# Output projection of an RG-LRU block with an expert-choice mixture: a third tile begun early, weight copies put later

## The chip, the cores and the metric

The kernel runs on one core of one Trainium2 chip. The time is that of the device, in microseconds (us), of the whole program from start to end. The engines are TensorE (PE: matmuls; PEld is its weight load), VectorE (DVE), ScalarE (ACT), GpSimd (POOL) and SyncE (SP), which here issues most of the DMA transfers. Each engine works off its own list of instructions in order, and waits on semaphores (counters) where it needs the work of another.

## What is computed

One layer: a bidirectional Griffin RG-LRU block on 1024 latent and 256 context tokens of width 1024, then an expert-choice mixture of 16 experts, then a norm. The part that matters here, cut from the reference:

```python
# rglru_mixer: g_lat, u_lat from h @ w_in; two directions of a gated linear recurrence
y_lat = 0.0
for d, reverse in enumerate(DIRECTIONS):
    ...
    y_lat = y_lat + diag_scan(jnp.exp(la_l), b_l, h_end, reverse)
out_lat = (jax.nn.gelu(g_lat) * y_lat).astype(h_lat.dtype) @ w_out      # (1024 x 1280) @ (1280 x 1024)
...
x = x + mod[:, 2] * y_lat                                               # gated residual
h = modulate(rms_norm(x, norm_ffn_g[l]), mod[:, 3], mod[:, 4])
x = x + mod[:, 5] * expert_choice_ffn(h, router_w[l], ...)              # router: softmax(h @ w_router), top 128 tokens of each expert
```

## The kernel before

Every fp32 product is made of three fp32r matmuls: high part by high part, low by high, high by low. "High" is the value rounded to fp32r (`copy` on ScalarE or a copy on GpSimd), "low" is what remains (a subtraction, mostly on VectorE).

**The mixer.** `mixer_block(n)` does channels 128n to 128n+127 (NB = 10 blocks) of all 1280 tokens: TensorE makes the input products and the gates, ScalarE the sigmoids, exp, tanh, square and square root, VectorE the convolution, the products and the scans. The result y of a block is split by `high_y` (ScalarE) and `low_y` (VectorE), and GpSimd's queue stores both to `y_scr` in HBM (`store_y`). For a block, VectorE's steps are: `i_d` times `u` for both directions (semaphore `v_done`), the w product for each direction (L960, `w_done`), `scan_input` for each (L987, `b_done`), `scans` (L994 to L1007: four scans, a sum, the product with the gelu).

**The output weight.** `a_w_out` comes as five pieces `wo_raw`, each for two blocks of channels. The high copies lie in `act_h` (four made by GpSimd, L496, `wo_h_ready`, the last by ScalarE), the low copies in `act_l`: `wo_low(i)` on VectorE (L970, semaphore `wo_l_ready`). In the list of VectorE `wo_low(0)` stands ahead of the w products of the last block, 1 and 2 behind each of them, 3 behind the scans, 4 behind the low part of the last y.

**The output projection** makes 8 tiles of 128 tokens (called tile 0 to tile 7), each in two halves of 512 columns in a PSUM bank each. `project_first` begins tiles 0 and 1, when y of eight blocks is stored: their y comes back from `y_scr` into `yt_first_h/l`. First the high products of both tiles (32 matmuls each: high y and low y by the high weight, L1392 and L1394), then the low products (high y by the low weight, 32 in all for both, L1399), then all three products of the ninth block (12 matmuls) and of the tenth (12), which takes y straight from `y_h` and `y_l`. Two `spread` matmuls put the gate row of the mixture (`gate5`) into banks 3 and 6. Tiles 2 to 7 follow in a loop, each 2 x 30 matmuls (`project_half`, L1376 to L1378), with y loaded by SP into `yt_h/l` (two slots) and x into `xt`. Between the halves of a tile stands the turning (8 transposes, L1424, `turn_tile`) of an earlier tile's normed rows, behind it the router product (16 matmuls, L1432, `route`).

For each tile VectorE gates and adds (L1030, L1032; `x2_ready`), ScalarE sums the squares and takes the root, VectorE scales (`scale_rows`, L1041, `xn2_ready`). SP's list holds per tile, in this order: store of the sum (`x_scr`), then, when the rows are scaled, store of the normed rows (`n_scr`), then the loads of the tile after the next. The loads of tile 3 stand behind the two stores of tile 0.

**The experts** stream 384 weight pieces of 1 MB, each split on ScalarE and VectorE and used by 12 matmuls.

Of the kernel before, what the change touches and what calls it, by code (L numbers as in the profile page):

```python
# [23 lines left out]
F32 = mybir.dt.float32  # L24
# [4 lines left out]
ALU = mybir.AluOpType  # L29
# [5 lines left out]
def program(nc, stack, x, c, ctx, c_ctx, ada_w, ada_b, norm_mix_g, norm_ffn_g, final_g, a_w_in, a_conv_w,  # L35
# [28 lines left out]
    def place(name, shape, dtype, kb):  # L64
# [154 lines left out]
        yt_first_loaded yt_second_loaded yt_ninth_loaded yt_loaded_a yt_loaded_b xt_loaded_a xt_loaded_b proj_done gated_done x2_ready sq2_done  # L219
        rms2_done rstd2_ready xn2_ready xn_turned h2T_ready h2T_second logits_done  # L220
# [62 lines left out]
    def wait_past(eng, signal, value):  # L283

        if not (isinstance(value, int) and value <= 0):
            eng.wait_ge(signal, value)

    with nc.Block() as block:
# [3 lines left out]
        def _(sp):  # L292
# [79 lines left out]
            def tile_loads(t, slot, early=False):  # L372
                if not early:
                    sp.wait_ge(sem["proj_done"], (t - 1) * 2)
                    sp.wait_ge(sem["x2_ready"], t - 1)
                cols = bass.ds(t * P, P)
# [4 lines left out]
                if early:  # L381
                    sp.wait_ge(sem["x2_ready"], t - 1)
                sp.dma_start(xt[slot][:], x[0, cols, :]).then_inc([sem["xt_loaded_a"], sem["xt_loaded_b"]][slot], 16)
# [14 lines left out]
            first_load(1, 1, 0, NB - 2, sem["yt_second_loaded"])  # L398
            sp.wait_ge(sem["y_stored"], 32 * (NB - 1))
# [8 lines left out]
            tile_loads(2, 0, early=True)  # L408
            tile_stores(0, 0)
            sp.wait_ge(sem["proj_done"], 4)  # L410
            tile_loads(3, 1, early=True)
# [165 lines left out]
        def _(act):  # L577
# [112 lines left out]
            def norm2(t, slot, j):  # L690
                act.wait_ge(sem["x2_ready"], t + 1)

                if j is not None:
                    act.wait_ge(n_stored[slot], j * 16)
                    act.wait_ge(sem["xn_turned"], t - 1)
                nc.scalar.activation(xn[slot][:], x2[slot][:], ACT.Square, accum_out=stat[:, 0, slot:slot + 1]).then_inc(sem["sq2_done"], 1)
                act.wait_ge(sem["sq2_done"], t + 1)
                nc.scalar.activation(stat[:, 1, slot:slot + 1], stat[:, 0, slot:slot + 1], ACT.Sqrt, scale=1.0 / D,
                                     bias=eps[:]).then_inc(sem["rms2_done"], 1)

            def modulate2(t):
                act.wait_ge(sem["xn_turned"], t + 1)
                wait_past(act, sem["logits_done"], t)
                for k in range(KD // 2):
                    last = nc.scalar.activation(h2T[:, k, :], bank(4 + k // 4)[:, (k % 4) * P:(k % 4 + 1) * P], ACT.Identity,
                                                scale=scale2[:, k:k + 1], bias=shift2[:, k:k + 1])
# [6 lines left out]
            act.wait_ge(sem["row_spread"], 4)  # L713
            for j in range(2):
                copy(gate5_row[:, j * HALF:(j + 1) * HALF], bank((3, 6)[j])).then_inc(sem["gate5_ready"], 1)
            modulate2(0)
            with act.Fori(1, NT // 2) as j:
                for slot in range(2):
                    t = j * 2 + slot
                    modulate2(t - 1)  # L720
                    norm2(t, slot, j)
# [79 lines left out]
            def squares(part):  # L801
                lo, hi = groups_fin[part]
                for t in range(lo, hi):
                    act.wait_ge(x_loaded[t], 32)
                    if t >= 2:
                        act.wait_ge(sem["squares_done"], NT + NCT + t - 1)
                    nc.scalar.activation(junk_fin[t % 2], fin[t][:], ACT.Square, accum_out=stat[:, 0, t:t + 1]).then_inc(sem["squares_done"], 1)
                act.wait_ge(sem["squares_done"], NT + NCT + hi)
# [14 lines left out]
            act.wait_ge(sem["squares_done"], NT + NCT + NT + 1)  # L823
# [5 lines left out]
        def _(dve):  # L829
# [84 lines left out]
            def mixer_block(n):  # L914
# [40 lines left out]
                if n == NB - 1:  # L955
                    wo_low(0)
                for d in range(2):
# [3 lines left out]
                    if n == NB - 1:  # L961
                        wo_low(1 + d)
# [56 lines left out]
            wo_low(3)  # L1019
            low_y(NB - 1)  # L1020
            wo_low(4)


            def residual(t, slot, j, turned=None):
                for half in range(2):
# [4 lines left out]
                    v.tensor_tensor(x2[slot][:, cols], bank(((0, 1), (2, 7))[slot][half]), gate2_row[:, cols], ALU.mult).then_inc(sem["gated_done"], 1)  # L1030
# [6 lines left out]
            def scale_rows(t, slot):  # L1037
                dve.wait_ge(sem["rms2_done"], t + 1)
                v.reciprocal(stat[:, 0, slot:slot + 1], stat[:, 1, slot:slot + 1]).then_inc(sem["rstd2_ready"], 1)
                dve.wait_ge(sem["rstd2_ready"], t + 1)  # L1040
# [598 lines left out]
```

## Time and profile before

| | us |
|---|---|
| median of 3 runs | 1716.64 (1716.53 to 1716.76) |
| profiled execution, its own time | 1717.74 |
| its span | 1716.0 |
| TensorE busy in the span | 1615.6 (94%) |
| VectorE busy | 1391.7 (81%) |
| ScalarE busy | 1212.4 (71%) |
| GpSimd busy | 223.1 (13%) |
| granted TensorE clock, mean | 0.97 |

All times below are from the span's start. The page of the profile gives totals by engine and by group of instructions; the timeline lists one engine's instructions with the idle time ahead of each and the instruction that ended it; the windows give busy time, granted clock and DMA share in a stretch. The granted clock is 1.00 at 2.4 GHz and 0.50 at 1.2 GHz.

### The profile page before, as it was taken

To read this page: it belongs to the slowest core of one execution; us is meant where nothing else is said; L and a number is where in the kernel's file an instruction comes from. 1 tells how busy PE (TensorE), PEld (TensorE's weight loads), DVE (VectorE), ACT (ScalarE), POOL (GpSimd) and SP (SyncE) were. 2 spreads that over 40 slices of the span, in tenths; PEclk is the share of its full clock that TensorE was granted. 3 is DMA by queue.
4 is the path that set the end of the run, shared out by engine and by line. 5 is a ranking of instruction groups with operands and counts; after the bars stand their busy time and mean duration, and the time that the engine had idled before them with its cause. 6 is when DMAs were issued, how large, how long until landed. Compare 5 with 4: busy or idle time off the path is not lost.

```text
span 1716.0 us, 21522 instructions
## 1 busy us (share of the span) xinstructions
PE 1615.6 (94%) x7661; PEld 1326.7 (77%) x7661; DVE 1391.7 (81%) x1115; ACT 1212.4 (71%) x1112; POOL 223.1 (13%) x154
## 2 busy tenths in 40 slices
PE   4999999997997389999999999999999999999995
PEld 1788888785886368888888888888888888888884
DVE  2777888789424879888898898988888989888896
ACT  3688888885213258778877777787777777877774
POOL 0400000003001300211202102102022021020010
PEclk9999999998998589999999999999999999999998
DMA  9323533434659169999999999999999999999995
GB/s 348 96 86 124 166 123 117 137 122 133 224 182 364 56 247 381 371 392 390 370 405 382 361 410 374 378 404 364 399 386 363 407 381 371 401 375 401 373 361 212
DMA packets 107654, 512.05 MB, mean 298 GB/s; under 512 B 11434, under 2 KB 37704, under 8 KB 56400
## 3 DMA queue, kind: packets, MB, share of 16 engines
q1 hardware_dynamic: 99968, 483.39, 72.3%
q0 software_dynamic: 7632, 27.92, 5.8%
q8 instruction: 36, 0.59, 0.1%
q14 instruction: 18, 0.15, 0.0%
HBM read 479.76 MB, written 31.52 MB: 298 GB/s over the span
## 4 chain that ended last, share of the span: by engine, by line
PE 87%; DVE 8%; SPq 2%; ACT 2%; issue 1%; DMA 0%; POOL 0%; ACTq 0%; DVEq 0%; POOLq 0%
PE psum L1500 14%; PE psum L1508 14%; PE psum L1502 14%; PE psum L1554 6%; PE psum L1561 6%; PE psum L1556 6%; PE psum L1268 5%; PE psum L1269 5%; PE psum L1270 5%; PE psum L1541 2%; PE psum L1376 2%; PE psum L1377 2%; PE psum L1378 2%; SPq L301 1%; DVE act_l L906 1%
## 5 line engine op out<-in xcount | busy, mean ns | idle before, releaser
L1155 DVE TENSOR_TENSOR part_l<-raw,part_h 128x2048 fp32r<-128x2048 f32 x380 | 847.6, 2286 | 58.0 <-ACT part_h L579 57.1
L579 ACT ACTIVATE part_h<-raw 128x2048 fp32r<-128x2048 f32 x384 | 720.7, 1917 | 165.7 <-PE psum L1508 94.8
L1500 PE MATMUL psum<-part_h,xgT_h 128*128 128x512 f32 x1024 | 287.3, 398 | 2.4 <-DVE xgT_l L1216 2.1
L1508 PE MATMUL psum<-part_l,xgT_h 128*128 128x512 f32 x1024 | 281.6, 392 | 0.1
L1502 PE MATMUL psum<-part_h,xgT_l 128*128 128x512 f32 x1024 | 281.7, 392 | 0.0
L1502 PEld LDWEIGHTS psum<-part_h,xgT_l 128*128 128x128 f32 x1024 | 194.1, 190 | 41.3
L1508 PEld LDWEIGHTS psum<-part_l,xgT_h 128*128 128x128 f32 x1024 | 193.3, 189 | 41.7 <-DVE part_l L1155 0.8
L1500 PEld LDWEIGHTS psum<-part_h,xgT_h 128*128 128x128 f32 x1024 | 191.1, 191 | 39.9 <-DVE xgT_l L1216 2.5
L1554 PE MATMUL psum<-part_h,hidT_h 128*128 128x512 f32 x512 | 157.9, 390 | 1.4 <-DVE hidT_l L1167 1.4
L1556 PE MATMUL psum<-part_h,hidT_l 128*128 128x512 f32 x512 | 157.7, 389 | 0.0
L1561 PE MATMUL psum<-part_l,hidT_h 128*128 128x512 f32 x512 | 136.9, 389 | 0.0
L539 POOL COPY id_scatter<-tok_id 128x1 int32 (+1 forms) x15 | 31.2, 2083 | 757.1 <-DVE y_out L1176 757.1
L1554 PEld LDWEIGHTS psum<-part_h,hidT_h 128*128 128x128 f32 x512 | 96.0, 188 | 21.7 <-DVE hidT_l L1167 1.8
L1561 PEld LDWEIGHTS psum<-part_l,hidT_h 128*128 128x128 f32 x512 | 96.1, 188 | 20.0
L1556 PEld LDWEIGHTS psum<-part_h,hidT_l 128*128 128x128 f32 x512 | 96.1, 188 | 19.9
L1268 PE MATMUL psum<-act_h,wu_h 128*128 128x512 f32 (+1 forms) x224 | 78.8, 352 | 1.3 <-DVE act_l L906 1.3
L579 ACT ACTIVATE hidT_h<-psum 128x512 fp32r<-128x512 f32 x64 | 35.0, 596 | 63.3 <-PE psum L1541 63.3
L1269 PE MATMUL psum<-act_h,wu_l 128*128 128x512 f32 (+1 forms) x224 | 78.8, 352 | 0.0
L1270 PE MATMUL psum<-act_l,wu_h 128*128 128x512 f32 (+1 forms) x224 | 78.7, 351 | 0.0
L1268 PE MATMUL psum<-act_h,wg_h 128*128 128x512 f32 x160 | 63.3, 396 | 0.0
L1269 PE MATMUL psum<-act_h,wg_l 128*128 128x512 f32 x160 | 62.4, 390 | 0.0
L1270 PE MATMUL psum<-act_l,wg_h 128*128 128x512 f32 x160 | 62.3, 389 | 0.0
(254 smaller groups left out, 2210.6 us busy)
## 6 DMA issues: line engine op xcount, KB each, us to landing
raw<-in_exp_w_gate_dram SPq DMA_DIRECT2D x128, 1024.0 KB, 7.1
raw<-in_exp_w_up_dram SPq DMA_DIRECT2D x128, 1024.0 KB, 6.8
raw<-in_exp_w_down_dram SPq DMA_DIRECT2D x128, 1024.0 KB, 9.4
ada_piece<-in_ada_w_dram SPq DMA_DIRECT2D x16, 1024.0 KB, 6.3
ada_buf<-in_ada_w_dram SPq DMA_DIRECT2D x8, 1024.0 KB, 12.9
u_raw<-in_a_w_in_dram SPq DMA_DIRECT2D x10, 512.0 KB, 3.8
g_raw<-in_a_w_in_dram SPq DMA_DIRECT2D x10, 512.0 KB, 8.5
y_scr<-y_h POOLq DMA_DIRECT2D x10, 512.0 KB, 3.8
```

The lines of the kernel that those rows point to most:

```text
L579: return nc.scalar.activation(dst, src, ACT.Identity)
L1155: v.tensor_tensor(part_l[slot][:], raw[slot][:], part_h[high][:].bitcast(F32), ALU.subtract).then_inc(sem["part_l_ready"], 1)
L1268: mm(out_ap, xh, wh, start=(i == 0), stop=False)
L1269: mm(out_ap, xl, wh, start=False, stop=False)
L1270: last = mm(out_ap, xh, wl, start=False, stop=(i == len(pairs) - 1))
L1376: mm(out_ap, yh, wo_h[:, n, cols], start=(n == 0), stop=False)
L1500: mm(dst, xgT_h[slot][:, i, :], wh[:, f, :], start=(i == 0), stop=False)
L1502: mm(dst, xgT_l[slot][:, i, :], wh[:, f, :], start=False, stop=False)
L1508: last = mm(dst, xgT_h[slot][:, i, :], wl[:, f, :], start=False, stop=(i == CHUNKS - 1))
L1554: mm(bank(4 + n), hh, wh[:, k, cols], start=(i == 0 and k == 0), stop=False)
L1556: mm(bank(4 + n), hl, wh[:, k, cols], start=False, stop=False)
L1561: last = mm(bank(4 + n), hh, wl[:, k, cols], start=False, stop=(i == CHUNKS - 1 and k == 1))
```

## The change

`project_first` now begins three tiles. Tile 2's high products of eight blocks (32 matmuls) stand behind those of tiles 0 and 1 and ahead of all low products; its 16 low products and its ninth and tenth blocks come behind the tenth block of tile 1. Tile 2 has banks 5 and 6 instead of 0 and 1 (`tile_banks`). SP loads its first eight blocks into `yt_h[0]`, `yt_l[0]` as soon as the scan inputs of the last block are made (these slots lie over the buffers that they read), the last two when all of y is stored. The turned rows go to banks 3 and 4. The spreads of the gate row go to bank 5, one in tile 4 and one in tile 5, and their copies on ScalarE with them. Router product 0 and the turning of tile 1 stand behind the first half of tile 3.

On VectorE `wo_low(0)` stands between the two w products, and `wo_low(1)` to `wo_low(4)` all behind the low part of the last y. Some semaphores are merged (`rms2_done` into `rms_done` and the like), and ScalarE's loop over the tiles is written out. The number of matmuls, copies and transferred bytes stays.

The core of the diff:

```diff
+    tile_banks = lambda t: (5, 6) if t == 2 else ((0, 1), (2, 7))[t % 2]
@@ SP @@
+            def third_load(lo, hi, loaded):
+                for part, dst in enumerate((yt_h, yt_l)):
+                    sp.dma_start(dst[0][:, lo:hi, :].bitcast(F32), y_scr[part, 2, :, lo:hi, :]).then_inc(loaded, 16)
...
             first_load(1, 1, 0, NB - 2, sem["yt_second_loaded"])
+            sp.wait_ge(sem["b_done"], 2 * NB)
+            third_load(0, NB - 2, sem["yt_third_loaded"])
...
             sp.wait_ge(sem["y_stored"], 32 * NB)
-            tile_loads(2, 0, early=True)
+            third_load(NB - 2, NB, sem["yt_third_rest"])
+            load_xt(2, 0)
             tile_stores(0, 0)
-            sp.wait_ge(sem["proj_done"], 4)
-            tile_loads(3, 1, early=True)
+            tile_loads(3, 1)
@@ VectorE, mixer_block @@
-                if n == NB - 1:
-                    wo_low(0)
                 for d in range(2):
...
-                    if n == NB - 1:
-                        wo_low(1 + d)
+                    if n == NB - 1 and d == 0:
+                        wo_low(0)
...
             scans(NB - 1)
-            wo_low(3)
             low_y(NB - 1)
-            wo_low(4)
+            for i in range(1, NB // 2):
+                wo_low(i)
@@ TensorE, behind project_first @@
-            for j in range(2):
-                spread(2 + j, bank((3, 6)[j]))
...
-            for t in range(2, NT):
+            turn_tile(0, 0)
+            for t in range(3, NT):
                 project_half(t, 0)
                 if t == 3:
-                    route(1)
-                if t == 2:
-                    turn_tile(0, 0)
-                else:
-                    turn_tile(t - 1, (t - 1) % 2)
-                project_half(t, 1)
-                if t == 2:
+                    pe.wait_ge(sem["gated_done"], 6)
                     route(0)
                     turn_tile(1, 1)
+                else:
+                    if t == 4:
+                        route(2)
+                    turn_tile(t - 1, (t - 1) % 2)
+                if t in (4, 5):
+                    wait_past(pe, sem["gate5_ready"], t - 4)
+                    spread(t - 2, bank(5))
+                project_half(t, 1)
+                if t == 3:
+                    route(1)
+                    turn_tile(2, 0)
                 else:
                     route(t - 1)
```

How it moves instructions is best seen in the lists of the engines. VectorE from the first w product of the last block to the last low weight copy, before (`act_l<-wo_raw` are the low weight copies, `y_l` the low parts of blocks nine and ten):

```order
L970 TENSOR_TENSOR act_l<-wo_raw_80,act_h 128x2048
L960 SCALAR_TENSOR_TENSOR t_fwd<-r_fwd,t_fwd 128x1280
L970 TENSOR_TENSOR act_l<-wo_raw_81,act_h 128x2048
L960 SCALAR_TENSOR_TENSOR t_bwd<-r_bwd,t_bwd 128x1280
L970 TENSOR_TENSOR act_l<-wo_raw_82,act_h 128x2048
...
L1007 TENSOR_TENSOR y<-y,t_fwd 128x1024
L970 TENSOR_TENSOR act_l<-wo_raw_83,act_h 128x2048
L1011 TENSOR_TENSOR y_l<-y,y_h 128x1024
L970 TENSOR_TENSOR act_l<-wo_raw_84,act_h 128x2048
```

and after:

```order
L971 SCALAR_TENSOR_TENSOR t_fwd<-r_fwd,t_fwd 128x1280
L981 TENSOR_TENSOR act_l<-wo_raw_80,act_h 128x2048
L971 SCALAR_TENSOR_TENSOR t_bwd<-r_bwd,t_bwd 128x1280
...
L1018 TENSOR_TENSOR y<-y,t_fwd 128x1024
L1022 TENSOR_TENSOR y_l<-y,y_h 128x1024
L981 TENSOR_TENSOR act_l<-wo_raw_81,act_h 128x2048
L981 TENSOR_TENSOR act_l<-wo_raw_82,act_h 128x2048
L981 TENSOR_TENSOR act_l<-wo_raw_83,act_h 128x2048
L981 TENSOR_TENSOR act_l<-wo_raw_84,act_h 128x2048
```

Four weight copies have gone to the end, and none stands between the last y and its low part any more.

SP's queue from the first loads of y to the loads of tile 3 (`yt_h_117`, `yt_l_119` are its slot; `yt_h_116`, `yt_l_118` that of tile 2), before:

```order
L370 DMA yt_first_l_123<-y_scr 128x128
L406 DMA xt_124<-in_x_dram 128x1024
L406 DMA xt_125<-in_x_dram 128x1024
L379 DMA yt_h_116<-y_scr 128x1280
L379 DMA yt_l_118<-y_scr 128x1280
L383 DMA xt_124<-in_x_dram 128x1024
L388 DMA x_scr<-x_0_126 128x1024
L390 DMA n_scr<-xn_128 128x1024
L379 DMA yt_h_117<-y_scr 128x1280
L379 DMA yt_l_119<-y_scr 128x1280
```

and after:

```order
L376 DMA yt_h_116<-y_scr 128x1024
L376 DMA yt_l_118<-y_scr 128x1024
...
L376 DMA yt_h_116<-y_scr 128x256
L376 DMA yt_l_118<-y_scr 128x256
L380 DMA xt_124<-in_x_dram 128x1024
L393 DMA x_scr<-x_0_126 128x1024
L395 DMA n_scr<-xn_128 128x1024
L386 DMA yt_h_117<-y_scr 128x1280
L386 DMA yt_l_119<-y_scr 128x1280
```

Tile 2's load is cut in two and its larger part stands ahead; the loads of tile 3 keep their place behind the store of tile 0's normed rows.

TensorE just ahead of tile 3 (its first matmul reads `yt_h_117`), before:

```order
L1378 MATMUL psum<-act_l,yt_h_116 128x512
L1432 MATMUL psum<-router,h2T 128x16 x8
L1424 MATMUL psum<-ident,xn_129 128x128 x8
L1376 MATMUL psum<-act_h,yt_h_117 128x512
L1377 MATMUL psum<-act_h,yt_l_119 128x512
```

and after:

```order
L1392 MATMUL psum<-act_h,yt_h_116 128x512
L1393 MATMUL psum<-act_h,yt_l_118 128x512
L1394 MATMUL psum<-act_l,yt_h_116 128x512
L1454 MATMUL psum<-ident,xn_128 128x128 x8
L1392 MATMUL psum<-act_h,yt_h_117 128x512
L1393 MATMUL psum<-act_h,yt_l_119 128x512
```

Before, tile 3 stood behind router product 0 and the turning of tile 1 (`xn_129`); now it stands behind the turning of tile 0 (`xn_128`), and those two come after its first half.

## Rows read from the trace of the kernel before

**Rows 1.** The page: its head and section 5's row of L1500.

```profile
span 1716.0 us, 21522 instructions
...
L1500 PE MATMUL psum<-part_h,xgT_h 128*128 128x512 f32 x1024 | 287.3, 398 | 2.4 <-DVE xgT_l L1216 2.1
```

**Rows 2.** Timeline of TensorE, 395 to 440: start, duration, instruction, count, [idle before, releaser].

```profile
398.58 1.22 PE L1392 MATMUL psum<-act_h,yt_first_h 128*128 128x512 f32 x2 [5.33 <-DMA yt_first_l<-y_scr]
...
415.31 5.60 PE L1399 MATMUL psum<-act_l,yt_first_h 128*128 128x512 f32 x24
...
427.85 3.78 PE L1399 MATMUL psum<-act_l,yt_first_h 128*128 128x512 f32 x8 [6.93 <-DVE act_l L970]
...
435.27 0.39 PE L1376 MATMUL psum<-act_h,y_h 128*128 128x512 f32 x1
...
438.10 1.13 PE L1355 MATMUL psum<-row_sum,ones_row 1*128 1x512 f32 x4
```

**Rows 3.** Windows of one microsecond: busy time of each engine, granted clock, DMA share, GB/s.

```profile
403.00:404.00 1.00, 1.00 (x6) 0.80 (x5) 1.00 (x1) 1.00 (x1) 1.00 (x1) 0.99 0.57 90
...
423.00:424.00 1.00, 0.00 (x0) 0.00 (x0) 0.97 (x2) 0.00 (x0) 0.00 (x0) 0.75 0.45 133
...
433.00:434.00 1.00, 1.00 (x4) 0.76 (x4) 0.00 (x0) 0.00 (x0) 0.00 (x0) 0.63 0.00 0
```

**Rows 4.** Timeline of VectorE, 402 to 437, columns as in rows 2.

```profile
402.27 3.98 DVE L970 TENSOR_TENSOR act_l<-wo_raw,act_h 128x2048 fp32r<-128x2048 f32 x1
...
406.18 1.48 DVE L960 SCALAR_TENSOR_TENSOR t_fwd<-r_fwd,t_fwd 128x1280 f32<-128x1280 f32 x1
...
407.58 2.28 DVE L970 TENSOR_TENSOR act_l<-wo_raw,act_h 128x2048 fp32r<-128x2048 f32 x1
...
413.39 1.48 DVE L987 TENSOR_TENSOR t_fwd<-t_fwd,i_fwd 128x1280 f32<-128x1280 f32 x1
...
417.33 0.68 DVE L994 TENSOR_TENSOR_SCAN t_fwd<-a_fwd,t_fwd 128x256 f32<-128x256 f32 x1
...
425.51 2.28 DVE L970 TENSOR_TENSOR act_l<-wo_raw,act_h 128x2048 fp32r<-128x2048 f32 x1
...
427.71 1.22 DVE L1011 TENSOR_TENSOR y_l<-y,y_h 128x1024 fp32r<-128x1024 f32 x1
...
428.85 2.28 DVE L970 TENSOR_TENSOR act_l<-wo_raw,act_h 128x2048 fp32r<-128x2048 f32 x1
...
436.27 0.69 DVE L1030 TENSOR_TENSOR x<-psum,gate_row 128x512 f32<-128x512 f32 x1 [5.14 <-PE psum L1378]
```

**Rows 5.** Timelines of GpSimd (POOL) and of ScalarE, 392 to 427.

```profile
392.23 11.89 POOL L496 TENSOR_SCALAR act_h<-wo_raw 128x2048 fp32r<-128x2048 f32 x4 [23.37 <-issue]
...
404.10 1.28 ACT L663 ACTIVATE r_bwd<-a_bwd 128x1280 f32<-128x1280 f32 x1
...
425.62 1.06 ACT L579 ACTIVATE y_h<-y 128x1024 fp32r<-128x1024 f32 x1 [4.03 <-DVE y L1007]
```

**Rows 6.** Timeline of TensorE, 456 to 466: tile 3's first half and what follows.

```profile
456.32 0.48 PE L1376 MATMUL psum<-act_h,yt_h 128*128 128x512 f32 x1
...
463.24 1.85 PE L1432 MATMUL psum<-router,h2T 128*128 128x16 f32 x16
...
464.94 1.07 PE L1424 MATMUL psum<-ident,xn 128*128 128x128 f32 x8
...
465.77 0.48 PE L1376 MATMUL psum<-act_h,yt_h 128*128 128x512 f32 x1
```

**Rows 7.** Timeline of SP's queue; then DMA issues with KB and us to landing.

```profile
443.73 0.79 SPq L379 DMA_DIRECT2D yt_l<-y_scr  x1
...
yt_l<-y_scr SPq DMA_DIRECT2D x1, 640.0 KB, 7.2
...
yt_l<-y_scr SPq DMA_DIRECT2D x1, 640.0 KB, 5.2
...
yt_first_h<-y_scr SPq DMA_DIRECT2D x1, 512.0 KB, 5.7
```

More of the change, by code:

```diff
@@ L712, in _, with gate5_half @@
             act.wait_ge(sem["y_stored"], 32 * NB)
-            act.wait_ge(sem["row_spread"], 4)
-            for j in range(2):
-                copy(gate5_row[:, j * HALF:(j + 1) * HALF], bank((3, 6)[j])).then_inc(sem["gate5_ready"], 1)
             modulate2(0)
[L717 to L721, printed above, removed]
+            norm2(2, 0, 1)
+            modulate2(1)
+            modulate2(2)
+            norm2(3, 1, 1)
+            def gate5_half(j):
+                act.wait_ge(sem["row_spread"], 3 + j)
+                copy(gate5_row[:, j * HALF:(j + 1) * HALF], bank(5)).then_inc(sem["gate5_ready"], 1)
+            for t in range(4, NT):
+                modulate2(t - 1)
+                if t < 6:
+                    gate5_half(t - 4)
+                norm2(t, t % 2, t // 2)
             nc.scalar.activation(soft[:, 0, 0:1], eps[:], ACT.Exp)
@@ L1370, in _ @@
                 mixer_block(n)
[L1372 removed]
+            out_bank = lambda t, half: bank(tile_banks(t)[half])
             def project(out_ap, yh, yl, n, half):
@@ L1382, in project_first, with low_part, ninth @@
                 cols = [slice(half * HALF, (half + 1) * HALF) for half in range(2)]
-                for t in range(2):
-                    pe.wait_ge([sem["yt_first_loaded"], sem["yt_second_loaded"]][t], 32)
+                yt = [(yt_first_h[0], yt_first_l[0]), (yt_first_h[1], yt_first_l[1]), (yt_h[0], yt_l[0])]
+                def low_part(tiles, n):
+                    for t in tiles:
+                        for half in range(2):
+                            mm(out_bank(t, half), yt[t][0][:, n, :], wo_l[:, n, cols[half]], start=False, stop=False)
+                def ninth(tiles):
+                    for t in tiles:
+                        for half in range(2):
+                            project(out_bank(t, half), yt[t][0][:, NB - 2, :], yt[t][1][:, NB - 2, :], NB - 2, half)
+                for t in range(3):
+                    pe.wait_ge([sem["yt_first_loaded"], sem["yt_second_loaded"], sem["yt_third_loaded"]][t], 32)
                     if t == 0:
@@ L1409, in project_first @@
                                 ).then_inc(sem["proj_done"], 1)
+                for n in range(NB - 2):
+                    low_part([2], n)
+                pe.wait_ge(sem["yt_third_rest"], 32)
+                ninth([2])
+                for half in range(2):
+                    project(out_bank(2, half), yt_h[0][:, NB - 1, :], yt_l[0][:, NB - 1, :], NB - 1, half
+                            ).then_inc(sem["proj_done"], 1)
             def project_half(t, half):
@@ L1413, in project_half @@
                 if half == 0:
-                    pe.wait_ge([sem["yt_loaded_a"], sem["yt_loaded_b"]][slot], t // 2 * 32)
+                    pe.wait_ge([sem["yt_loaded_a"], sem["yt_loaded_b"]][slot], (t - 1) // 2 * 32)
                 pe.wait_ge(sem["gated_done"], (t - 2) * 2 + half + 1)
                 for n in range(NB):
-                    last = project(out_bank(slot, half), yt_h[slot][:, n, :], yt_l[slot][:, n, :], n, half)
+                    last = project(out_bank(t, half), yt_h[slot][:, n, :], yt_l[slot][:, n, :], n, half)
                 last.then_inc(sem["proj_done"], 1)
```

83 lines of the change are left out of this document (39 added, 44 removed).

## The prediction

> **What bounds the kernel now.** I read the page first: 1716.0 us of span, and in the expert stage TensorE's commonest matmul sits idle only 2.4 us before 1024 instructions [rows 1]. So the expert stage runs at TensorE's pace, and a microsecond saved or lost ahead of it should reach the end. Next the timeline of TensorE at the end of the mixer [rows 2]. After the gates it waits 5.33 us for the first tiles of y, does the high products of tiles 0 and 1 (until 415.31), then 24 low products in 5.60 us. Now comes the hole that the change aims at: 6.93 us of idle until 427.85, because the fourth low copy of the output weight is not there. Then 32 matmuls, which at the 0.23 us each of the 24 would take 7.4 us, last from 427.85 to 438.10. The windows say why [rows 3]: the granted clock falls inside the hole (0.75 in 423 to 424) and is whole again only within 433 to 434 (0.63); so some 5.9 us of this work ran at 1.2 GHz instead of 2.4. After the first wait it was the same: half from 398.58 until 403 (0.99 in the next microsecond), 4.4 us. A matmul of 512 columns costs twice as much at half clock, so these two stretches lost 2.9 and 2.2 us.
>
> The reader then wants to know who TensorE waits for: VectorE, which is busy without a gap from 402.27 to 431.13 [rows 4]. From 438 on TensorE is the bound: tile 2 needs no wait, tile 3 starts at 456.32 right behind other work [rows 6]. The loads of tile 3 are issued at 443.73 and land 7.2 us later, at 450.9 [rows 7]. They have **5.4 us of slack**. This slack is what the change eats.
>
> **VectorE's part.** No copy is removed; the order changes. At 402.27 stands a low copy that took 3.98 us where its like takes 2.28: it was held up for 1.70 us, and in that time POOL is in its own high copies, which end at 404.1 [rows 4, 5]. Now the w product of direction 0 stands there, and I give it the same hold: 402.27 + 1.70 + 1.40 (start to start, 406.18 to 407.58) = 405.4. Low copy 0 adds 2.20 (407.58 less the next start, as 425.51 to 427.71): 407.6. The w product of direction 1 needs ScalarE's square, which begins at 404.10 and takes 1.28 [rows 5], so no wait: 409.0. The stretch from the scan inputs to the first scan took 3.94 (413.39 to 417.33): 412.9. The scans, sum and product took 8.18 (417.33 to 425.51): 421.1, against 425.5 before. The last low part of y now comes straight behind, and must wait for ScalarE's high part, 1.06 [rows 5], plus a tenth for two hand-overs; before, a weight copy covered that. So 422.25, and the low part (1.14, 427.71 to 428.85) ends at 423.4. Four weight copies follow, 3 x 2.20 + 2.28 = 8.9: **432.3, against 431.13**. The last weight copy is 1.15 us later than before; only the low part of y is earlier.
>
> **TensorE's part until tile 1 is done.** The high products of tile 2 need its first eight blocks. Their load waits for the scan inputs, whose buffers it overwrites: SP can issue at 409.0 + 2.8 = 411.8, the second half at 412.2. How long it takes no row shows; the three early loads took up to 5.7 us, a pair by itself 5.2, and the pair of tile 3, in a crowd, 7.2 [rows 7]. Two stores of y lie beside it, much as a third load lay beside the early ones, so I take 5.7: 417.9 (bounds 417.4 and 419.4). TensorE is out of work at 415.5 and idles 2.4 us. In the hole of before, work ended at 420.9 and the clock fell in the middle of 423 to 424 [rows 3], some 2.6 us later, so I expect it to hold, barely. Then 32 high and 32 low products at 0.23: 432.7, just behind the 432.3 of VectorE, whose copies are each there in time for their turn. Blocks nine and ten (24 matmuls at 0.236, from 435.27 to 438.10 for twelve) now run at full clock: the tenth starts at 435.5 against 435.27, and tile 1 is done at **438.4 against 438.10**. The hole is full, but with work of tile 2, and its end is where it was.
>
> **Behind it.** Of tile 2 only 28 matmuls are left, 6.6 us, so TensorE is through with it at 445.0, and after the turning of tile 0 (0.83) at 445.8. Then it asks for tile 3. SP issues that load behind the store of tile 0's normed rows, and these hang on the chain that starts with tile 0's projection: VectorE at 436.27 to SP at 443.73 [rows 4, 7]. Nothing in that chain is shortened, its start moves by 0.25. So the load is issued at 444.0 and lands at 451.2; TensorE starts tile 3 at 451.3 after 5.5 us of idle. That is 5.0 us earlier than 456.32. The idle is as long as the one before 398.58, so I take its price for the clock as well: 2.2 us. Left: 2.8 us. But before, at this point, three things were already done that now come later: router product 0 (1.70), the turning of tile 1 (0.83) and the two spreads of the gate row (1.1, the row at 438.10) [rows 2, 6]: 3.6 us. From there both kernels have the same work with TensorE as the bound: normed rows, router inputs and loads of tiles 4 to 7 come by my count 4 us or more ahead of their use. Sum: -5.0 + 2.2 + 3.6 = **+0.8 us**. The span of 1716.0 becomes 1716.8. The profiled execution took 1717.74 in all, 1.7 more than its span and 1.1 more than the median of the runs, 1716.64; profiling costs both kernels alike, so I put the sum on the median: **1717.4**.
>
> A rule speaks here about one term. Tile 3's pair of loads took 7.2 us to its end. The Trainium skill, DMA: Bandwidth & Descriptors (the part on the two cost components), gives a transfer about 2.0 us fixed and its bytes at 436 GB/s beside that; the pair of 1.31 MB would by this estimate be there 5.0 us after its first issue, near 448.5, and the sum would be about -1.9 us. The trace does not agree for this pair, since stores and the next input rows share the queues.
>
> **Rivals.**
> (a) The loads of tile 3 are quick, 5.2 us, as those of tile 2 were [rows 7]. Start at 449.3: -7.0 + 2.2 + 3.6 = -1.2, 1715.4. If the clock also holds through 3.5 us of idle, -3.4, 1713.2. For it: one pair did it. Against: its neighbours, which in the changed kernel are the same as before. Chance 0.12, of that 0.03 with the clock. The rule of the page named above points this way.
> (b) Tile 3 needs no wait at all, as one who looks only at the hole would count: start at 445.8, -10.5 + 3.6 = -6.9, 1709.7. The order of SP's queue speaks against it. 0.02.
> (c) The clock falls in the early idle of 2.4 us. Then 2.2 us are lost there, VectorE no longer covers any of it, and tile 0's chain starts later by as much: +3.0, 1719.6. 0.16.
> (d) Slower: tile 2's first load takes 7.2 us like the pair of tile 3. It lands at 419.4, TensorE idles 3.9 us, the clock falls (about 2.5 lost), and the tenth blocks start 4.0 us later: +4.8, 1721.4. It decides when the landing is over 1.5 us later than I take and the clock falls with it. 0.10.
> My forecast has 0.58. About 0.02 is left for what I don't see.
>
> **Numbers.** A measurement of this kernel can tell about 0.2% from no change, 3.4 us: 1713.2 and 1720.1. Faster by more: (b) and a part of (a), 0.05. Slower by more: (d) and the upper edge of (c), 0.15. Within: 0.80. The range takes in the forecast, the slow-clock form of (a) and (c), with half a microsecond on either side for how long a half-clock stretch lasts (4.4 or 5.9 us): 1714.8 to 1720.3.
>
> **What would show it.** In the changed trace: VectorE's last weight copy ends near 432.3; TensorE idles 2 to 3 us near 416 with the clock at 1.0; tile 1's last product near 438.4; then one idle of 5 to 6 us before tile 3, put down to a DMA of yt_l, with the clock at 0.5 behind it; and the router product of tile 6 ends within 2 us of where it did. I am wrong if the wait before tile 3 is under 3 us, if SP issues its load before 443, or if waits appear at tiles 4 to 7.

## The result, and the profile after

| | before | after |
|---|---|---|
| median of the runs | 1716.64 us (5 runs, 1716.13 to 1717.56) | 1724.60 us (5 runs, 1722.35 to 1725.03) |
| profiled execution | 1717.74 us | 1722.35 us |
| its span | 1716.0 us | 1720.6 us |
| TensorE busy | 1615.6 us | 1615.5 us |
| granted clock, mean | 0.97 | 0.971 |

The change makes the kernel slower by a factor of 1.004, interval 1.003 to 1.0051: 8 us by the medians, where I forecast 0.8. It lies outside my range. The traced execution of the changed kernel is the shortest of its five, and that of before lies 1.1 us above its median, so the two traces differ by only 4.6 us. The last experiment looks for the rest, and does not find all of it.

First TensorE, in the timeline of the changed kernel from 395 to 510 (start, duration, instruction, count, idle before it and who ended it). These rows answer to [rows 2] and [rows 6].

```profile
398.61 1.22 PE L1421 MATMUL psum<-act_h,yt_first_h 128*128 128x512 f32 x2 [5.32 <-DMA yt_first_l<-y_scr]
...
419.47 0.74 PE L1421 MATMUL psum<-act_h,yt_h 128*128 128x512 f32 x2 [3.84 <-DMA yt_l<-y_scr]
...
428.50 7.42 PE L1404 MATMUL psum<-act_l,yt_first_h 128*128 128x512 f32 x32
...
441.19 3.79 PE L1404 MATMUL psum<-act_l,yt_h 128*128 128x512 f32 x16
...
447.54 1.03 PE L1454 MATMUL psum<-ident,xn 128*128 128x128 f32 x8
...
455.09 0.80 PE L1392 MATMUL psum<-act_h,yt_h 128*128 128x512 f32 x1 [6.51 <-DMA yt_l<-y_scr]
...
463.37 1.85 PE L1462 MATMUL psum<-router,h2T 128*128 128x16 f32 x16
...
484.97 1.12 PE L1371 MATMUL psum<-row_sum,ones_row 1*128 1x512 f32 x2
...
502.57 1.12 PE L1371 MATMUL psum<-row_sum,ones_row 1*128 1x512 f32 x2
```

The hole of 6.93 us is gone, and two waits have taken its place: 3.84 us ahead of tile 2 and 6.51 us ahead of tile 3, both for y from `y_scr`. Tile 1 is done at 441.19, where it was done at 438.10. The first half of tile 3 ends where router product 0 starts, 463.37; before, that half ended at 463.24, with router product 0 and the turning of tile 1 already done. The last two rows are the spreads, each now by itself.

VectorE, same columns, answers to [rows 4]; it did what was forecast to a tenth of a microsecond:

```profile
402.30 3.18 DVE L971 SCALAR_TENSOR_TENSOR t_fwd<-r_fwd,t_fwd 128x1280 f32<-128x1280 f32 x1
...
422.36 1.22 DVE L1022 TENSOR_TENSOR y_l<-y,y_h 128x1024 fp32r<-128x1024 f32 x1 [1.12 <-ACT y_h L586]
...
423.50 8.89 DVE L981 TENSOR_TENSOR act_l<-wo_raw,act_h 128x2048 fp32r<-128x2048 f32 x4
...
439.45 0.69 DVE L1041 TENSOR_TENSOR x<-psum,gate_row 128x512 f32<-128x512 f32 x1 [7.06 <-PE psum L1394]
```

Its last weight copy ends at 432.39, and its first sum of tile 0 comes 3.18 us later than the 436.27 of before. SP's queue and the DMA issues (KB, us from issue to landing; the first four rows of issues in 405 to 422, the last two in 438 to 458), beside [rows 7]:

```profile
411.95 0.33 SPq L376 DMA_DIRECT2D yt_h<-y_scr  x1
412.32 0.43 SPq L376 DMA_DIRECT2D yt_l<-y_scr  x1
...
446.92 0.79 SPq L386 DMA_DIRECT2D yt_l<-y_scr  x1
```

```profile
y_scr<-y_h POOLq DMA_DIRECT2D x1, 512.0 KB, 6.8
yt_h<-y_scr SPq DMA_DIRECT2D x1, 512.0 KB, 4.2
yt_l<-y_scr SPq DMA_DIRECT2D x1, 512.0 KB, 7.1
y_scr<-y_l POOLq DMA_DIRECT2D x1, 512.0 KB, 6.7
...
yt_h<-y_scr SPq DMA_DIRECT2D x1, 640.0 KB, 5.9
yt_l<-y_scr SPq DMA_DIRECT2D x1, 640.0 KB, 8.1
```

Tile 2's load was issued when I said, and took 7.1 us, not 5.7. GpSimd's stores of the ninth block of y (issued at 411.66 and 413.36) are in flight with it. Tile 3's load was issued 3.2 us later than before and took 0.9 us longer. Windows of one microsecond (busy time of each engine, granted clock, DMA share, GB/s), beside [rows 3]:

```profile
418.00:419.00 1.00, 0.00 (x0) 0.00 (x0) 0.97 (x2) 0.00 (x0) 0.00 (x0) 1.00 1.03 393
...
420.00:421.00 1.00, 1.00 (x4) 0.75 (x4) 0.99 (x1) 0.00 (x0) 0.00 (x0) 0.70 0.00 0
...
423.00:424.00 1.00, 1.00 (x4) 0.77 (x4) 1.00 (x2) 0.00 (x0) 0.63 (x2) 0.60 1.16 260
```

The DMA engines are full when the load lands, and the clock falls after the idle stretch, when TensorE works again, and is back 3.4 us of half clock later.

### The profile page after: what moved, and what is told of

It reads as the page before. It is cut to its first block, busy times and chain, and to the rows that moved or that the text cites. A ratio compares the mean times of both kernels' runs of the same rounds, so it can differ in the third digit from the quotient of the medians.

```text
span 1720.6 us, 21501 instructions
## 1 busy us (share of the span) xinstructions
PE 1615.5 (94%) x7661; PEld 1326.0 (77%) x7661; DVE 1391.7 (81%) x1115; ACT 1212.4 (70%) x1112; POOL 230.8 (13%) x154
## 4 chain that ended last, share of the span: by engine, by line
PE 86%; DVE 7%; SPq 2%; ACT 2%; issue 1%; DMA 1%; POOL 0%; ACTq 0%; DVEq 0%; POOLq 0%
PE psum L1534 14%; PE psum L1542 14%; PE psum L1536 14%; PE psum L1595 6%; PE psum L1588 6%; PE psum L1590 6%; PE psum L1284 5%; PE psum L1285 5%; PE psum L1286 5%; PE psum L1575 2%; PE psum L1392 1%; PE psum L1394 1%; PE psum L1393 1%; SPq L303 1%; DVE act_l L919 1%
```

## The experiments

Twelve runs in three groups, each on a chip of its own and with its own runs of the kernel before (medians 1717.50, 1717.25 and 1717.31 us). Where a time is set against the changed kernel without more, that is its 1724.02 us in the first group; for a run of a later group the difference then goes across chips. My theory from the traces: the change costs three things, the late landing of tile 2's first load, the wait for tile 3 behind tile 0's stores, and the spreads taken apart; the copy order on VectorE is innocent. The rival: the copies put late hold up the end of tile 1.

**The same kernel again.** No edit.

> The changed kernel once more, for a second profile, since its five times spread from 1722.35 to 1725.03 and the profiled one was the fastest. My theory of the loss: (1) the first load of tile 2 lands about 1.5 us later than I took, TensorE idles about 3.9 us and its clock falls; (2) the wait for tile 3's load, about 6.5 us, with half clock behind it; (3) each spread of the gate row alone costs about 1.2 us where the two together cost 1.1. It expects these three again, and the rest of the spread in the lengths of the half-clock stretches (mean granted clock 0.96 to 0.97), not in another wait. A rival puts it in another wait, which would show as an idle time of TensorE over 1 us between 395 and 545 that the first profile has not. Time 1722 to 1725.

1724.02 us (1722.44 to 1724.78, 5 runs), ratio 1.004, interval 1.0025 to 1.0054. The loss repeats: 6.5 us by the medians. Its timeline:

```profile
419.69 0.74 PE L1421 MATMUL psum<-act_h,yt_h 128*128 128x512 f32 x2 [3.56 <-DMA yt_l<-y_scr]
...
453.52 0.80 PE L1392 MATMUL psum<-act_h,yt_h 128*128 128x512 f32 x1 [6.33 <-DMA yt_l<-y_scr]
```

The same two waits. But here the clock did not fall behind the first: 1.00 in every window from 405 to 451. An idle of 3.6 to 3.8 us lowers the clock in one execution and not in another.

**Only the copy order.** The kernel before, with VectorE's new order and nothing else:

```diff
-                if n == NB - 1:
-                    wo_low(0)
...
-                    if n == NB - 1:
-                        wo_low(1 + d)
+                    if n == NB - 1 and d == 0:
+                        wo_low(0)
...
-            wo_low(3)
             low_y(NB - 1)
-            wo_low(4)
+            for i in range(1, NB // 2):
+                wo_low(i)
```

> The kernel before with one part of the change alone: the low weight copies in the new order on VectorE (the first between the two w products, four behind the low part of the last y). Tile 2 is not begun early. My theory: VectorE's last copy ends 1.2 us later than 431.1, TensorE does 8 low products, idles some 8 us till the second copy at 425.7, and is done with tile 1 about 1 us later than 438.1. Slower by 0.5 to 2 us: 1717.2 to 1718.7. The rival, that the later weight copies are what costs the 8 us: 1721 or more.

1718.10 us (1717.54 to 1719.56, 10 runs), ratio 1.0008, interval 0.9998 to 1.0017. One longer hole:

```profile
425.98 7.23 PE L1397 MATMUL psum<-act_l,yt_first_h 128*128 128x512 f32 x24 [9.19 <-DVE act_l L968]
...
446.57 1.03 PE L1422 MATMUL psum<-ident,xn 128*128 128x128 f32 x8
```

The steps up to the router product of tile 6 come 0.5 us later than before (438.58 against 438.10, 538.56 against 538.08). By the medians the copy order alone costs 0.6 us, by the interval 2.9 at most: it can't be what costs the 6.5.

**Only the third tile.** The changed kernel with the old copy order (the edit above, backwards).

> The changed kernel with the other part alone: three tiles begun early, but VectorE's low copies in the order of before. My theory: the scan inputs are done at 416.2 instead of 411.9, so the load of tile 2 is issued 4.3 us later and lands about 422 to 423.5; TensorE idles 7 us or more, its clock falls, tile 1 is done about 443 to 446 and tile 3 waits for its load all the same. Slower than the changed kernel by 3 to 5 us: 1726 to 1729. The rival (the later copies cost the time): faster than the changed kernel, 1717 to 1721.

1726.91 us (1725.26 to 1728.53, 4 runs), ratio 1.0053, interval 1.0036 to 1.007. The two waits are there again (5.60 and 5.99 us), and tile 1 is done at 444.29:

```profile
421.31 1.22 PE L1423 MATMUL psum<-act_h,yt_h 128*128 128x512 f32 x2 [5.60 <-DMA yt_l<-y_scr]
```

The first wait is shorter than the 7 us or more that I gave, because this load took only 4.5 us; the run with less traffic comes back to that. So the loss comes with the third tile, and the new copy order takes 3 us of it back. In this trace a lone spread started at 488.06, and the clock fell 0.9 us later:

```profile
489.00:490.00 1.00, 1.00 (x3) 0.67 (x3) 0.54 (x2) 1.00 (x3) 0.00 (x0) 0.50 0.90 371
```

**Tile 3's y ahead of tile 0's stores.** The changed kernel, where SP loads tile 3's y as soon as `proj_done` is 4 (tile 1's last product), ahead of x for tile 2 and of tile 0's stores:

```diff
             third_load(NB - 2, NB, sem["yt_third_rest"])
+            load_yt(3, 1)
             load_xt(2, 0)
             tile_stores(0, 0)
-            tile_loads(3, 1)
+            load_xt(3, 1)
```

> The changed kernel with the loads of tile 3's y issued as soon as tile 1 is projected, ahead of x for tile 2 and of tile 0's two stores in SP's queue. My theory: issue near 441.3 instead of 446.5, landing near 449, TensorE waits at most 1 us instead of 6.5 and keeps its clock there. Faster than the changed kernel by 6 to 8 us: 1716 to 1718.5, near the kernel before or under it. A rival: the queues are full at that time, so that the gain is eaten by later stores and by x for tile 2, and the time stays within 2 us of the changed kernel.

1715.85 us (1712.65 to 1717.46, 10 runs), ratio to before 0.9988, interval 0.9978 to 0.9998; 8.2 us faster than the changed kernel of the same group. The load is issued at 442.62 and 443.00 and lands after 6.1 us, at 449.1; the wait for tile 3 is gone, and router product 0 starts at 456.67 instead of 463.37. One wait is left:

```profile
419.58 1.22 PE L1425 MATMUL psum<-act_h,yt_h 128*128 128x512 f32 x2 [4.76 <-DMA yt_l<-y_scr]
```

Of the three costs, each mended by itself, the place of this load in SP's queue is the largest, and mending it is enough to be no slower than before.

**The clock's part.** The changed kernel with dummy matmuls in both idle stretches:

```diff
+                    if t == 2:
+                        for i in range(16):
+                            mm(out_bank(2, i % 2), wo_h[:, 0, 0:P], wo_h[:, 0, cols[i % 2]], start=True, stop=True)
...
+            pe.wait_ge(sem["gated_done"], 2)
+            for i in range(27):
+                mm(bank(i % 2), wo_h[:, 0, 0:P], wo_h[:, 0, (i % 2) * HALF:(i % 2 + 1) * HALF], start=True, stop=True)
```

> The changed kernel with dummy matmuls that keep TensorE busy in its two idle stretches: 16 of 512 columns ahead of tile 2's first product (into banks that tile 2 overwrites), 27 ahead of tile 3 (into banks 0 and 1 once tile 1 is read). Nothing that is computed changes, no load moves. Theory that the clock behind the two waits costs about 1.7 and 1.4 us: the granted clock stays at 1.0 from 410 to 460, and the kernel is about 3 us faster than the changed one, near 1721 (span 1717 to 1718). Rival, that the late loads alone set the time and the clock gives nothing (the half-clock stretches are made up later, where TensorE waits anyway): no difference to the changed kernel, 1724; and if the dummies hold up the real products, slower.

1719.44 us (1717.96 to 1723.55, 11 runs), ratio 1.0019, interval 1.001 to 1.0028; 4.6 us under the changed kernel, where 3 were expected. Its span of 1717.7 is what I gave.

```profile
415.62 3.79 PE L1414 MATMUL psum<-act_h 128*128 128x512 f32 x16
419.68 0.73 PE L1424 MATMUL psum<-act_h,yt_h 128*128 128x512 f32 x2 [0.27 <-DMA yt_l<-y_scr]
...
446.90 6.39 PE L1474 MATMUL psum<-act_h 128*128 128x512 f32 x27
453.90 0.50 PE L1392 MATMUL psum<-act_h,yt_h 128*128 128x512 f32 x1 [0.60 <-DMA yt_l<-y_scr]
...
460.83 1.85 PE L1465 MATMUL psum<-router,h2T 128*128 128x16 f32 x16
```

The clock stays at 1.00 from 404 to 542. From tile 2's first product to the end of tile 1 it takes 439.76 - 419.68 = 20.08 us, against 441.19 - 419.47 = 21.72 in the changed kernel: the clock cost 1.6. Tile 3's half takes 460.83 - 453.90 = 6.93, against 8.28: 1.35. Tile 2's load lands no earlier; tile 3's, whose chain starts with tile 0, lets its half start 1.2 us earlier. At router product 0 (460.83 against 463.37) both together are worth 2.5 us. What is left is the loads and the spreads.

**Tile 2's first load in earlier parts.** Its buffers come free one after the other, and each part now starts when the buffer below it does:

```diff
+            sp.wait_ge(sem["w_done"], 2 * NB)
+            third_part(1, 0, 6, sem["yt_third_loaded"])
+            sp.wait_ge(sem["b_done"], 2 * NB - 1)
+            third_part(0, 0, NB - 2, sem["yt_third_loaded"])
             sp.wait_ge(sem["b_done"], 2 * NB)
-            third_load(0, NB - 2, sem["yt_third_loaded"])
+            third_part(1, 6, NB - 2, sem["yt_third_loaded"])
```

> The changed kernel with tile 2's first load in smaller parts that start when the buffers below them are free: blocks 0 to 5 of the low part behind the w products (issued near 409.0), the high part behind the first scan input (410.4), the rest behind the second (412). Theory, that the late landing of this load (419.5) is the first of the two costs: it lands at 415 to 416, TensorE idles at most 1 us ahead of tile 2, the clock holds, tile 1 is done near 438.5 instead of 441.2, and the kernel is 3 to 3.5 us faster than the changed one, near 1721. The wait ahead of tile 3 stays. Rival, that the queues are full there and the landing is set by the traffic, not by the issue: the load lands near 419 whatever its issue, and the time is 1724.

1721.00 us (1718.18 to 1721.66, 11 runs), ratio 1.002, interval 1.0011 to 1.0028: 3 us under the changed kernel, as the theory says.

```profile
415.89 0.73 PE L1428 MATMUL psum<-act_h,yt_h 128*128 128x512 f32 x2
...
425.92 6.54 PE L1411 MATMUL psum<-act_l,yt_first_h 128*128 128x512 f32 x24 [0.65 <-DVE act_l L988]
...
450.12 0.79 PE L1399 MATMUL psum<-act_h,yt_h 128*128 128x512 f32 x1 [4.64 <-DMA yt_l<-y_scr]
```

Tile 2 starts at 415.89 with hardly an idle, and the bound there is now VectorE's copies, by 0.65 us. Tile 3 starts 5 us earlier, since its chain starts with tile 0. But behind the lone spread at 480.88 the clock falls (0.50 in 483 to 485), and from router product 0 to that of tile 6 it takes 81.51 us instead of 79.92. Of the 4.1 us gained at router product 0, 2.5 are left there.

**Both spreads together**, in the idle ahead of tile 3, in banks 0 and 1:

```diff
+            pe.wait_ge(sem["gated_done"], 2)
+            for j in range(2):
+                spread(2 + j, bank(j))
...
-                if t in (4, 5):
-                    wait_past(pe, sem["gate5_ready"], t - 4)
-                    spread(t - 2, bank(5))
```

> The changed kernel with both spreads of the gate row together in the idle ahead of tile 3 (banks 0 and 1), as the kernel before had them together, instead of one in tile 4 and one in tile 5. Theory that each lone spread costs TensorE 1.2 us in a stretch where it is the bound, and nothing in the idle: 2.4 us faster than the changed kernel, near 1721.6; the router product of tile 6 ends 2.4 us earlier at the same wait ahead of tile 3. Rival, that they are hidden behind other waits: no difference, 1724.

1720.38 us (1716.16 to 1724.09, 12 runs), ratio 1.0018, interval 1.001 to 1.0027: 3.6 us under the changed kernel by the medians, where I gave 2.4, but its runs spread over 8 us.

```profile
449.31 1.13 PE L1372 MATMUL psum<-row_sum,ones_row 1*128 1x512 f32 x4
455.18 0.80 PE L1393 MATMUL psum<-act_h,yt_h 128*128 128x512 f32 x1 [4.74 <-DMA yt_l<-y_scr]
```

Each spread is two instructions. Four take 1.13 us here; in tile 4 and again in tile 5 two alone take 1.12. The timeline of the kernel before, asked for in windows under half a microsecond, shows why:

```profile
438.10 0.70 PE L1355 MATMUL psum<-row_sum,ones_row 1*128 1x512 f32 x2
438.63 0.59 PE L1355 MATMUL psum<-row_sum,ones_row 1*128 1x512 f32 x2
```

The first instructions of both spreads start at 438.10, their second ones at 438.63: the two run side by side, each with its operands on its own partition (32j in `spread(j)`). From router product 0 to that of tile 6: 541.39 - 463.99 = 77.40 us, against 543.29 - 463.37 = 79.92. The lone spreads cost 2.5 us at full clock; here they stand in a wait and cost nothing.

**The three mends together.**

> The changed kernel with three mends together: tile 3's y loaded ahead of tile 0's stores, as in the run with that alone (8.2 us faster than the changed kernel); tile 2's first load in earlier parts; both spreads together behind tile 2's products. If the three costs are separate, about 8.2 + 3 + 1 to 2.4: near 1711, 5 to 7 us faster than the kernel before. Rival: with the loads of tile 3 earlier TensorE no longer waits and what is saved at the front is met by the next late thing (tile 0's normed rows for the turning, the router's inputs or xt), and the time stays near 1716.

**1709.93 us** (1708.72 to 1710.21, 5 runs), ratio to before 0.9957, interval 0.9944 to 0.997: 7.3 us faster than before, a version that beats both.

```profile
416.08 0.73 PE L1433 MATMUL psum<-act_h,yt_h 128*128 128x512 f32 x2 [0.35 <-DMA yt_l<-y_scr]
...
426.15 6.54 PE L1416 MATMUL psum<-act_l,yt_first_h 128*128 128x512 f32 x24 [0.71 <-DVE act_l L993]
...
453.69 1.85 PE L1474 MATMUL psum<-router,h2T 128*128 128x16 f32 x16
```

No wait over 0.8 us between 400 and 532, and no half clock between 404 and 536. Router product 0 starts at 453.69: 9.7 us earlier than in the changed kernel. The gain on the changed kernel, 14.1 us by the medians, is a little more than the 12.2 to 13.6 that I added up.

**Less traffic beside tile 2's first load.** Of the ninth block of y only tiles 0 and 1 are stored at its place; for the others values of the tenth are written there later, so this kernel computes a wrong result and serves for its time alone:

```diff
+                    tiles = 2 if n == NB - 2 else NT
-                    pool.dma_start(y_scr[part, :, :, n, :]...
+                    pool.dma_start(y_scr[part, 0:tiles, :, n, :]...
...
+            for part, buf in enumerate((y_h, y_l)):
+                pool.dma_start(y_scr[part, 2:NT, :, NB - 2, :]...
```

> The changed kernel with less traffic beside tile 2's first load: of the ninth block of y only tiles 0 and 1 are stored at its place (2 x 128 KB instead of 2 x 512); for tiles 2 to 7 values of the tenth block are written into the ninth's place behind the last stores, so the y of those tiles is wrong in that block, and the bytes are the same. The issue of the load stays at 411.9 and 412.3. Theory, that the load took 7.1 us because two stores of 512 KB share the queues with it: it now lands at 417.0 to 417.8, after 5 to 5.5 us (a pair by itself took 5.2), the early idle is 1.5 to 2.3 us, the clock holds there, tile 1 is done near 438.5, and the kernel is 1.5 to 3 us faster than the changed one. Rival, that the load is slow for another reason (its own pattern of rows, or reads behind writes to the same scratch): 7.1 us again and no gain.

1720.58 us (1718.66 to 1723.50, 10 runs), ratio 1.002, interval 1.001 to 1.0029: 3.4 us under the changed kernel, where I gave 1.5 to 3.

The DMA issues in 405 to 422, and TensorE's waits:

```profile
yt_l<-y_scr SPq DMA_DIRECT2D x1, 512.0 KB, 5.1
...
y_scr<-y_h POOLq DMA_DIRECT2D x1, 128.0 KB, 4.5
```

```profile
417.49 0.74 PE L1424 MATMUL psum<-act_h,yt_h 128*128 128x512 f32 x2 [2.11 <-DMA yt_l<-y_scr]
...
450.67 0.79 PE L1395 MATMUL psum<-act_h,yt_h 128*128 128x512 f32 x1 [5.20 <-DMA yt_l<-y_scr]
```

Issued at the same time, the load lands after 5.1 us instead of 7.1, with 768 KB less beside it. So the load's own pattern of rows, half of the rival, is out. The other half, reads behind writes to the same scratch, isn't separated here, since fewer bytes are also fewer writes. The run with only the third tile has a row on it:

```profile
yt_l<-y_scr SPq DMA_DIRECT2D x1, 512.0 KB, 4.5
```

There the same load was issued at 416.37 and 416.74, behind a full store of y (issued at 413.91, landed after 3.9 us) and ahead of the other (417.77). It too read behind a write still in flight, and was the quickest of the three (7.1, 5.1, 4.5); what it lacked was both stores beside it from the start. The idle is 2.11 us and the clock holds through it, as I had forecast for an idle of 2.4. Router product 0 comes 4.2 us earlier than in the changed kernel; behind the lone spreads 3.2 of it is lost again in this trace, in 6.8 us at half clock from 481 to 489.

**The first two mends without the third**: tile 3's y ahead, tile 2's load in parts, the spreads apart.

> The changed kernel with tile 3's y ahead of tile 0's stores and with tile 2's first load in earlier parts, the spreads left one in tile 4 and one in tile 5. All three mends gave 1709.9. If the lone spreads cost what the run with that mend alone gained over the changed kernel (3.6 to 4.2), this one gives 1713.5 to 1714; if they cost only their own 2.5 us in the timelines, 1712.4. Rival, that the mends are not separate and the third gave nothing here: 1710.

1710.47 us (1709.69 to 1711.42, 5 runs), ratio 0.9964, interval 0.9949 to 0.9978. Both figures of my theory missed; this is the rival's. The timelines of the two kernels differ by 1.3 us at router product 6 (532.40 against 531.08) and not by 2.5, because with all three mends there is no idle stretch left to put the spreads in: together they stand on the path for 1.06 us, and apart they cost 2.5. And the first two mends are worth more together (13.6 us under the changed kernel) than the sum of each (8.2 + 3.0): the one alone still had half clock from 418 to 426, the other alone the wait of 4.64 us.

**Two more traces of the changed kernel.**

> The changed kernel as it is, for its trace alone. Its two profiled executions were the shortest of their runs (1722.35 and 1722.44; the others took 1723.1 to 1725.0), so the traces miss up to 2.5 us. Theory, that the rest is clock: in some executions a further stretch at half clock of 3.4 us lies behind a lone spread in tile 4 or 5, as in two traces of variants (483 and 489), or both early waits are followed by one; each such stretch costs 1.7 us. Expected in a run of 1724 or more: half clock between 475 and 510 or 6.8 us instead of 3.4 near 420. Rival: a wait that the other traces don't show.

> The same kernel once more, for a second trace, with the same expectation: the total time goes up by 1.7 us for each further 3.4 us at half clock between 396 and 546, and by nothing else.

1724.56 and 1722.27 us. Their waits for tile 3 and, in the second, a window behind the lone spread at 481.64:

```profile
455.40 0.80 PE L1392 MATMUL psum<-act_h,yt_h 128*128 128x512 f32 x1 [6.96 <-DMA yt_l<-y_scr]
```

```profile
451.49 0.50 PE L1392 MATMUL psum<-act_h,yt_h 128*128 128x512 f32 x1 [4.78 <-DMA yt_l<-y_scr]
```

```profile
485.00:486.00 1.00, 1.00 (x4) 0.80 (x3) 0.00 (x0) 0.00 (x0) 0.00 (x0) 0.50 0.00 0
```

The expectation is half wrong. The further half-clock stretch in tile 4 exists, but it stands in the shorter of the two runs. The longer one has about as much half clock between 396 and 546 as the first trace of the changed kernel (16.8 and 17.0 us) and is 2.2 us longer in span. Tile 3's load took 8.6 us here (8.1, 7.9 and 6.4 in the others) and its half started 0.3 us later; the half-clock stretch there lies from 453 to 461 instead of 451 to 458, so more of it falls on work, another 1.0; and 0.9 are added behind the router product of tile 6, with the lower mean clock (0.963 against 0.971). So the traces of one kernel differ by clock stretches and by the landing of one crowded load. The experts start at 596.87, 595.97, 597.78 and 595.17 in the four traces of the changed kernel, against 591.01 in the one of before: 4.2 to 6.8 us later. From there to the end the four take 1123.7, 1124.7, 1125.0 and 1125.4 us, against 1125.0 before: the 1.3 us by which the first trace seems better at the end lie within that scatter. Why the medians differ by 8 us in the first runs and by 6.5 in the second isn't settled.

## Why the prediction was wrong

I compare with the first trace of the changed kernel, step by step, up to the router product of tile 6.

| step | forecast | measured |
|---|---|---|
| VectorE's last weight copy ends | 432.3 | 432.39 |
| tile 2's first load issued | 411.8, 412.2 | 411.95, 412.32 |
| its landing | 417.9 | 419.4 |
| TensorE idle ahead of tile 2 | 2.4 | 3.84 |
| clock there | holds | falls (3.4 us at half) |
| tile 1 done | 438.4 | 441.19 |
| turning of tile 0 starts | 445.0 | 447.54 |
| last load of tile 3 issued | 444.0 | 446.92 |
| tile 3 starts | 451.3 | 455.09 |
| clock loss behind it | 2.2 | 1.35 |
| router product 0, turning of tile 1 | 2.53 | 2.53 |
| spreads | 1.1 | 2.55 |
| router product of tile 6 against before | +0.8 | +5.21 |

**Right:** VectorE's part to a tenth; that the hole only moves; that tile 3 waits for a load whose place in SP's queue hangs on tile 0's chain; that an idle of about 2.4 us leaves the clock alone (one trace, with 2.11); that no wait arises at tiles 4 to 7; that both kernels run at TensorE's pace from tile 3 on.

**The first failed step is "I take 5.7".** I had bounds of 417.4 and 419.4 and took a value near the lower one, because "two stores of y lie beside it, much as a third load lay beside the early ones". That is a miscount. Beside the early loads lay one more load: three in all. Here lay two stores beside two loads: four transfers of 512 KB, on DMA engines that the windows show full from 415 on at 393 to 410 GB/s. The upper bound was the right value. With 768 KB less beside it the same load took 5.1 us. The Trainium skill, DMA: Bandwidth & Descriptors (the two cost components), gives one transfer, by a fit to DMAs issued from GpSimd, about 2.0 us and its bytes at 436 GB/s. For the pair's own 1.05 MB the estimate is 4.4 us, which the trace contradicts. If one puts in all the bytes that are in flight together, which is my reading and not the page's, the estimate for 2.10 MB is 6.8 us, where the trace has 7.1, and for 1.31 MB it is 5.0, where the run with less traffic has 5.1. In the run with only the third tile the windows add up to about 1.4 MB from the issue to the landing; the estimate is 5.2 and the trace has 4.5. So the sum of bytes tells the crowded load from the other two, and misses one of those by 0.7 us.

This is my rival (d), to which I gave 0.10: the landing at 419.4, an idle of 3.84 instead of 3.9, the clock falling. Its price came out a little lower (tile 1 3.1 us later, not 4), yet the whole ended above its 1721.4, for two more reasons.

**The second is tile 3's start**, 3.8 us later than forecast: 3 from the chain, which started 3.2 us late with tile 0, and 0.9 because the load took 8.1 us instead of 7.2. I called 5.4 us of slack what the change eats, and took the chain in front of it as fixed. It isn't: any lateness ahead of tile 0's end moves this load by the same amount, so the early idle is paid here once more. The clock gave 0.85 back: part of the half-clock stretch (451 to 458) lay in the idle itself.

**The third is the spreads.** I counted "1.1" for the two together, though the change puts one in tile 4 and one in tile 5. By itself each takes 1.05 us from its start to the next one's (484.97 to 486.02) and 0.2 more at the matmuls around it, 2.5 for the two. Together they run side by side for 1.06 us; taking them apart doubles the price. The sum of the misses is 3.8 - 0.85 + 1.45 = 4.4, which is 5.21 less 0.8. From the router product of tile 6 to the experts the changed kernel loses another 0.65 us (596.87 against 591.01) and wins 1.3 in them, which gives the 4.6 between the spans. The medians are 8 us apart; the 3.4 us between the two figures are not accounted for step by step.

**What no row of before showed** is the clock behind a lone spread: in four of the ten traces with the spreads apart it fell between 481 and 493, and in none of the four traces without. What stands there in a row is router product, turning and spread, 3.8 us of narrow work. That the lone spread tips it is an inference from these counts; it wasn't varied by itself at that place, and four traces without are few.

The chances were wrong too: I had two unknown landings, one with its bounds 2 us apart, and gave 0.58 to the case in which both come out well.

## What to carry to other kernels

Work that is pulled forward into a hole brings its operands' transfers with it. Before counting the hole as filled, add up every byte in flight from the issue to the landing, stores of other engines among them, and expect the landing by that sum and not by the load's own bytes. Then look at what hangs behind the filled hole in each queue: here one load, moved ahead of two stores that it has nothing to do with, turned 0.4% slower into no loss, and with the early load cut into parts that start as their buffers come free, into 0.4% faster than before. Leave together small matmuls that run side by side.

## What the runs showed of the hardware

The half-clock stretches that begin and end between 396 and 546 lasted about 3.4, 6.8 or 10.2 us in all fourteen traces, and their place against the idle that precedes them varies: after 3.84 us of idle the clock fell about a microsecond after work had begun again (0.70 in 420 to 421), with 2.99 us in another kernel it had fallen already when work began (0.61 in 418 to 419, work from 419.20), and with 3.56 and 3.33 us it did not fall at all. Half clock is thus not a fixed price of an idle of 3 to 4 us but a chance; with 2.11 us, in one trace, it did not come. It may be one reason why executions of one kernel differ: the twelve with the spreads together lie within 8 us, the five of each of the two best kernels, with no idle over 0.8 us there, within 1.5 and 1.7.

The DMA engines moved 393 to 410 GB/s with loads and stores mixed. Of the four transfers of 512 KB that shared them, three took 6.7 to 7.1 us, also the store that was issued first; only the first load was through in 4.2. Two fp32 matmuls with one row each, on partitions of their own, ran side by side: 1.06 us for both and 1.05 for one alone.
